# One mixer's scan pipelined by direction, with weight rounding on GpSimd and its remainder on VectorE

## The reference

```python
def step(s, inp):                       # one chunk of one head, one direction
    qc, kc, vc, gc = inp                # gc = log_sigmoid(z) / 16
    b = jnp.cumsum(gc, axis=2)
    b_last = b[:, :, -1:, :]
    q_dec = qc * jnp.exp(b)
    scores = jnp.where(mask, q_dec @ (kc * jnp.exp(-b)).T, 0.0)
    o = scores @ vc + q_dec @ s
    s_new = jnp.exp(b_last).T * s + (kc * jnp.exp(b_last - b)).T @ vc
    return s_new, o
```

```python
g = (gates.reshape(B, T, 4, HEADS) + b_gate).transpose(2, 0, 3, 1)
# log_i = g[0], g[2];  log_f = log_sigmoid(g[1]), log_sigmoid(g[3])
```

## Time and profile before

| | |
|---|---|
| median of 3 runs (lowest, highest) | 3000.23 us (2997.96, 3006.75) |
| the profiled execution | 3005.11 us, span 3003.2 us, mean granted TensorE clock 0.951 |
| TensorE busy | 2759.6 us, 92% of the span |
| VectorE, ScalarE, GpSimd busy | 1296.2, 986.0, 1001.6 us |
| first GLA projections start, scan of GLA head 0 starts | about 1603 us, about 1660 us |
| TensorE takes up the second half's scan | 2068.5 us |
| branch products begin | about 2350 us |

### The profile page before, as it was taken

How to read it: one execution, slowest core, us unless ns; L and a number is a source line. 1 busy time by engine, 2 the same in 40 slices (tenths; PEclk the granted TensorE clock), 3 DMA queues, 4 the chain that set the end, 5 groups by cost and what they waited for, 6 DMA issues and landing times.

```text
span 3003.2 us, 35461 instructions
## 1 busy us (share of the span) xinstructions
PE 2759.6 (92%) x13958; PEld 2141.7 (71%) x13958; DVE 1296.2 (43%) x1755; ACT 986.0 (33%) x1652; POOL 1001.6 (33%) x683
## 2 busy tenths in 40 slices
PE   7988999999999799999998888596998999899997
PEld 6866658887797574888876666465876565688886
DVE  2758445443354863544333344526333212333322
ACT  5468422222344872222223344322222100222221
POOL 5565403436545660134562322411220223200000
PEclk9999999999999999999998999797998999899998
DMA  5230024554422002355452111011111331233322
GB/s 127 91 65 1 19 70 119 148 134 133 140 75 84 18 1 59 104 137 139 133 145 66 43 29 42 28 29 28 43 43 42 80 88 57 65 104 95 88 87 67
DMA packets 386053, 230.39 MB, mean 77 GB/s; under 512 B 9340, under 2 KB 382204, under 8 KB 385888
## 3 DMA queue, kind: packets, MB, share of 16 engines
q1 hardware_dynamic: 383408, 224.09, 27.1%
q0 software_dynamic: 1952, 1.94, 0.8%
q10 hardware_dynamic: 528, 2.10, 0.2%
HBM read 226.01 MB, written 2.10 MB: 76 GB/s over the span
## 4 chain that ended last, share of the span: by engine, by line
PE 73%; DVE 9%; ACT 8%; DMA 6%; issue 2%; POOL 0%; SPq 0%; DVEq 0%; ACTq 0%; POOLq 0%
PE ps L815 63%; PE scores L815 7%; DMA raws<-in_w_down 5%; PE ps L957 1%; ACT wH L1770 1%; DVE R L2058 1%; DVE R L2316 1%; ACT R L1895 0%; DVE spare L2068 0%; ACT U L1609 0%; DMA ring<-in_w_in 0%; DVE R L2314 0%; DVE QK_parts L2048 0%; ACT spare L1632 0%; DVE R L2356 0%
## 5 line engine op out<-in xcount | busy, mean ns | idle before, releaser
L815 PE MATMUL ps<-xH,wH 128*128 128x512 f32 x1000 | 396.9, 397 | 8.3 <-DVE xL L2227 8.3
L815 PE MATMUL ps<-xL,wH 128*128 128x512 f32 x1000 | 391.3, 391 | 0.0
L815 PE MATMUL ps<-xH,wL 128*128 128x512 f32 x1000 | 390.9, 391 | 0.0
L1770 ACT ACTIVATE wH<-raws 128x2048 fp32r<-128x2048 f32 (+1 forms) x114 | 192.9, 1692 | 503.8 <-PE ps L815 307.3
L2253 DVE TENSOR_TENSOR wL<-raws,wH 128x2048 fp32r<-128x2048 f32 (+1 forms) x113 | 233.7, 2068 | 286.4 <-ACT wH L1770 286.3
L815 PE MATMUL ps<-ring_parts,U_parts 128*128 128x256 f32 (+1 forms) x1936 | 311.7, 290 | 12.8 <-DVE ring_parts L2110 6.2
L716 POOL TENSOR_TENSOR spare<-spare,cvec 128x1024 f32<-128x1024 f32 x64 | 124.5, 1946 | 563.6 <-DMA spare<-in_w_ada 563.6
L815 PE MATMUL ps<-R 128*64 128x128 f32 (+6 forms) x1768 | 276.6, 344 | 29.3 <-DVE R L2334 4.6
L815 PEld LDWEIGHTS ps<-ring_parts,U_parts 128*128 128x128 f32 x1936 | 277.7, 197 | 25.9 <-issue 22.6
L815 PEld LDWEIGHTS ps<-R 128*64 128x64 f32 (+2 forms) x1768 | 171.3, 166 | 131.1 <-issue 77.0
L768 POOL CAST ring_parts<-ring 128x2048 fp32r<-128x2048 f32 x28 | 54.6, 1951 | 547.5 <-DMA ring<-in_w_in 540.5
(11 more groups left out here) (408 smaller groups left out, 4697.5 us busy)
## 6 DMA issues: line engine op xcount, KB each, us to landing
raws<-in_w_gate_up SPq DMA_DIRECT2D x88, 512.0 KB, 5.5
ring<-in_w_in SPq DMA_DIRECT2D x34, 1024.0 KB, 5.9
spare<-in_w_ada SPq DMA_DIRECT2D x64, 512.0 KB, 4.1
raws<-in_w_down SPq DMA_DIRECT2D x32, 704.0 KB, 6.1
raws<-in_w_ffn_in SPq DMA_DIRECT2D x44, 512.0 KB, 5.1
ring<-in_w_in SPq DMA_DIRECT2D x22, 512.0 KB, 6.0
raws<-in_w_ffn_out SPq DMA_DIRECT2D x16, 704.0 KB, 4.5
ring<-in_w_o SPq DMA_DIRECT2D x6, 896.0 KB, 5.4
```

Of the source, the lines that this page charges most:

```text
L815: return nc.tensor.matmul(o, a, b, start=first, stop=last)
L1770: ap.do(f(wH[:, g % 2, 0:n], raws[:, g % 2, 0:n], ACT.Copy), wh_ready)
```

## The change

It has two parts.

**The decays of a direction are made during the scan of the one before.** `decays` is cut into `decay_sums` and `decayed`, `decay_exponents` into `decay_logs` and `decay_exponents`. In direction 0 of head h the decay inputs of (h, 1) go to TensorE behind the key transposes, and in direction 1 those of (h+1, 0). `q`, `k`, `v` 0 to 2 of the next head now lie in direction 0, and `v` 3 to 5 and both `gate` in direction 1, ahead of the outputs. `head_outputs` of head h-1 moves into direction 0 of head h, behind its second decay input; that of head 3 behind `q`, `k`, `k` of head 4. The decays of (0, 0) are made inside head 0's `v` projections. The minimum and the subtraction become one instruction.

**The gate rows of the second half** are biased, and their logarithms taken, on 16 x 768 before they are picked apart, inside direction 1 of head 3; the picked rows are then only copied.

**GpSimd only rounds (`round_piece`), and VectorE subtracts (`second_low`)** for pieces 1 to 23, at places written into VectorE's order; piece 0, the two small pieces and the branch and output pieces stay with GpSimd whole. GpSimd reorders five tiles and VectorE three.

The core of the diff; left out are names of semaphores and the places of scratch rows:

```diff
+            def round_piece(j):
+                i = PLACE[j]
...
+                pg.do(nc.gpsimd.tensor_copy(high, raw_), second_high)
...
             def gla_scan(h, d, nxt):
                 _, _, v_, _ = head(h)
+                last_head = h == NH2 - 1
...
                 key_transposes(kd[:, d, :])
                 transposed = ab.n
-                run(nxt("v", (2, 5)[d]))
+                if d == 0:
+                    decay_inputs(h, 1)
+                    if h > 0:
+                        head_outputs()
+                    run(nxt("v", 0) if last_head else nxt("q"))
+                    beside_states = nxt("v", 1) if last_head else nxt("k", 1)
+                elif last_head:
+                    pe.wait_ge(gates_split, 1)
+                    parts_job(ab, lambda b: b[0:16, 0:256], small(GATES_AT, 16), XcP)
+                    parts_job(ab, lambda b: b[0:16, :], small(GATES_AT, 16), XP)
+                    beside_states = nxt("gate", 0)
+                else:
+                    decay_inputs(h + 1, 0)
+                    run(nxt("v", 3))
+                    beside_states = chain(nxt("v", 4), nxt("v", 5))
                 pe.wait_ge(a_free, transposed)
...
+                if d == 0 and last_head:
+                    pp.more(u_permuted, 2)
+                    for m in range(2, 6):
+                        run(nxt("v", m))
+                elif d == 0:
+                    run(nxt("k", 0))
+                    for m in range(3):
+                        run(nxt("v", m))
+                elif last_head:
+                    run(nxt("gate", 1))
+                    pe.wait_ge(gates_logged, 1)
...
+                else:
+                    run(nxt("gate", 0))
+                    run(nxt("gate", 1))
...
             for h in range(NH2):
                 n_ = h + 1
...
+                if h > 0:
+                    head_norm(gla_squares)
+                keys_by_token(kdt)
+                decay_logs(h, 1)
                 if n_ < NH2:
...
+                    evacuate(n_, ("q", 0), ("k", 1), ("k", 0))
+                    decay_exponents(h, 1)
+                    evacuate(n_, ("v", 0), ("v", 1), ("v", 2))
...
+                if n_ < NH2:
+                    decay_logs(n_, 0)
+                    evacuate(n_, ("v", 3), ("v", 4), ("v", 5))
+                    decay_exponents(n_, 0)
+                    evacuate(n_, ("gate", 0), ("gate", 1))
...
+            def second_low(name, h):
+                j = SECOND.index((name, h))
+                raw_, high, low = place_parts(PLACE[j])
+                dve.wait_ge(second_high, j)
+                vp.do(v.tensor_tensor(low, raw_, high.bitcast(F32), ALU.subtract), piece_split)
...
+            second_low("v", 0)
+            decay_sums(0, 0)
+            decayed(0, 0)
+            second_low("gate", 0)
+            second_low("qk", 1)
             for h in range(NH2):
-                decays(h, 0)
+                vp.more(dec_ready)
+                masked(0)
+                if h > 0:
+                    head_outputs(h - 1, 3, Y)
+                second_low("v", h + 1)
                 if h == NH2 - 1:
...
                     for k in range(POOL_TILES, KT):
                         permute(vp, v, k, og_row)
                     vp.also(u_permuted)
...
+                states(gla_order(0), ST, DV, lambda c: dec[:, 0, c:c + 1])
+                decay_sums(h, 1)
+                decayed(h, 1)
+                if h == NH2 - 1:
+                    second_low("gate", NH2)
+                gla_outputs(0)
+                vp.more(dec_ready)
+                masked(1)
+                states(gla_order(1), ST, DV, lambda c: dec[:, 1, c:c + 1])
+                if h + 1 < NH2:
+                    second_low("gate", h + 1)
+                    decay_sums(h + 1, 0)
+                    decayed(h + 1, 0)
+                    if h + 2 < NH2:
+                        second_low("qk", h + 2)
+                else:
...
+                    second_low("qk", NH2)
+                gla_outputs(1)
+                vp.also(og_ready)
...
             rows(0)
+            head_outputs(NH2 - 1, 3, Y)
+            second_low("qk", NH2 + 1)
...
             rows(1)
+            second_low("v", NH2 + 1)
...
+                if d == 1 and h + 1 < NH2:
+                    second_low("gate", NH2 + h + 1)
...
                 if h + 1 < NH2:
+                    if h > 0:
+                        second_low("v", NH2 + h + 1)
                     convolve(h + 1)
                 for d in range(2):
                     mlstm_outputs(h, d)
+                vp.also(og_ready)
                 head_outputs(h, 4, YM)
+                if h + 2 < NH2:
+                    second_low("qk", NH2 + h + 2)
```

More of the change, by code:

```diff
@@ L779, in _ @@
             split_small(lr_in, LR_AT, 2 * RANK, lr_split)
[L780 to L784, removed]
+            def round_piece(j):
+                i = PLACE[j]
+                landed[i] += 16 * len(second_dmas(j))
+                pool.wait_ge(piece_in[i], landed[i])
+                raw_, high, _ = place_parts(i)
+                pg.do(nc.gpsimd.tensor_copy(high, raw_), second_high)
+            for j in range(1, SECOND.index(("gate", NH2))):
+                round_piece(j)
+                if j == 3:
+                    split_small(gates_in, GATES_AT, 16, gates_split)
             pool.wait_ge(head_in, NH2)
@@ L788, in _ @@
             pg.also(u_permuted)
-            for j in range(SECOND.index(("gate", NH2)), len(SECOND)):
+            for j in range(SECOND.index(("gate", NH2)), N_PROJ):
+                round_piece(j)
+            for j in range(N_PROJ, len(SECOND)):
                 split_piece(j)
@@ L1906, in _ @@
                 if n_ < NH2:
-                    evacuate(n_, ("k", 1))
-                evacuate(n_, ("v", 0), ("v", 1))
-                keys_by_token(kdt)
-                evacuate(n_, ("v", 2), ("v", 3), ("v", 4))
-                keys_by_token(kdt)
-                evacuate(n_, ("v", 5), ("gate", 0))
-                head_norm(gla_squares)
-                evacuate(n_, ("gate", 1))
-            act.wait_ge(y_ready, NH2)
-            bank = ab.take(act)
-            copy_out(G16[:, 0:256], bank[0:16, 0:256], a_free)
@@ L1920, in _ @@
-            bank = ab.take(act)
-            copy_out(G16[:, 256:768], bank[0:16, :], a_free)
-            evacuate(NH2, ("q", 0))
+                    evacuate(n_, ("q", 0), ("k", 1), ("k", 0))
+                    decay_exponents(h, 1)
+                    evacuate(n_, ("v", 0), ("v", 1), ("v", 2))
+                else:
+                    evacuate(n_, ("v", 0), ("v", 1))
+                    decay_exponents(h, 1)
+                    evacuate(n_, *[("v", m) for m in range(2, 6)])
+                keys_by_token(kdt)
@@ new lines, in _ @@
+                if n_ < NH2:
[3 more added lines that the diff above has]
+                    evacuate(n_, ("gate", 0), ("gate", 1))
+            for a, n in ((0, 256), (256, 512)):
+                bank = ab.take(act)
+                ap.do(f(G16[:, a:a + n], bank[0:16, 0:n], ACT.Identity, bias=bgate[:, 0:1]), a_free)
+            ap.do(f(LF16, G16, ACT.Abs))
+            ap.do(f(LF16, LF16, ACT.Exp, scale=-1.0))
@@ L1923, in _ @@
+            ap.do(f(LF16, LF16, ACT.Ln, bias=ones[0:16, 0:1]), gr_ln)
+            evacuate(NH2, ("gate", 0))
+            evacuate(NH2, ("gate", 1))
             for g in range(4):
@@ L1953, in _ @@
                 if h > 0:
-                    beside(("q", 0), ("k", 0), ("k", 1))
+                    beside(("q", 0))
+                    beside(("k", 0), ("k", 1))
                 beside(("v", 0))
```

113 lines of the change are left out of this document (47 added, 66 removed).

## The result

| | median (lowest, highest) | runs |
|---|---|---|
| before | 2999.1 us (2993.36, 3006.75) | 4 |
| after | 2962.44 us (2958.03, 2965.5) | 4 |

The ratio of after to before is 0.9875, with a 95% interval of 0.9849 to 0.9901: 36.7 us faster by the medians, 30 to 45 by the interval. Some 5 of the 47.0 lie where nothing was changed: the mixers begin 2.7 us earlier in the trace of after (1572.3 for 1575.0), and what follows the second half's scan is 2.0 us shorter.

What follows compares the result with a forecast made beforehand. TensorE, busy 92% of the span, was held by 86 us of waits between 1590 and 2070 us. Removing 82, adding 44 and regaining 12 by clock gives 50 us: 2955 from the profiled execution, 2950 against the median, range 2920 to 2984.

Steps and rivals of the forecast that it cites:

- The forecast case: Whole kernel: the named waits go and the listed smaller ones come, giving 2935 to 2972 us; chance 0.62.
- signs of being wrong: VectorE waiting for rounded pieces with states or outputs behind, clock staying at 0.92, or second half losing over 7 us.
- Waits removed: TensorE's waits: `q` 26.6 us, head 3's tiles 29.9, gate rows 22.2, and 3.3 of the opening's 7.4; together 82.0.
- Waits added before the gate rows: Opening 5 us, `v` of head 1 1.3, `head_outputs` 8, `gate`'s low part 2, head 3 11, gate rows 9.6.
- the tiles: Head 3, before the states: VectorE's three tiles take 11 us, so TensorE waits 6.3 us.
- The clock's 12 us: Heads 0 to 3 and behind the gate rows: work at 1.2 GHz speeds up, at most 14.5 us, taken as 12.
- The second half's 7 us: Second half: `q` twice waits for a low part behind `head_outputs`, 3.5 us each, 7 added.
- A: Added small waits are covered; only `head_outputs` (8) and the second half's `q` (7) remain: 81 us gained, 2920; chance 0.13.
- Rival B: VectorE and GpSimd hold each other up: 23 low parts each 1.9 us late, 44 lost, 2994; half, 2972; chance 0.14.
- C: Late loads stop the scan through VectorE's order: 2.2 us per piece uses up the gain, 4 gives 3042; chance 0.06.
- D: Decays still end last because VectorE reaches them only after the states: 3000 us; chance 0.05.
- The subtraction over 768 columns: On VectorE: 0.96 us everywhere in the profile after, where before it took 3.79 beside GpSimd's subtraction.

Runs made afterwards that it cites:

- e5: The changed kernel with only the second half's low part of `qk` moved ahead of `head_outputs`: 2945.73 us, ratio to before 0.9814.
- e9: e2 with only the second half's low part of `qk` moved ahead of `head_outputs`: 2981.45 us, ratio to before 0.9921.
- e1: The changed kernel, but GpSimd rounds and subtracts every piece and VectorE makes no low part: 2969.41 us, ratio to before 0.99.
- e2: The kernel before, old scan order, but GpSimd only rounds pieces 1 to 23 and VectorE subtracts: 2991.12 us, ratio to before 0.9965.
- e8: The changed kernel plus e5's edit, head 0's `v` 0 to 2 emptied before the first decay's exponents, and all eight tiles on GpSimd: 2939.94 us.
- e7: The changed kernel with ScalarE copying the transposed keys before the head norm in heads 1 to 3: 2973.11 us, ratio to before 0.9899.

## Why the prediction was right, and where its sum was off

**Range and sign.** 2950 was forecast, 2920 to 2984; it is 2962.4. The forecast case (2935 to 2972) holds: the waits it named went, and new ones came where it put them. But 37 to 41 us came of 50, and the sum came near by two errors that cancelled, which is luck. Two of its own signs of being wrong are there: the second half lost more than 7 us, and VectorE did wait for rounded pieces with states behind it, though that cost TensorE only 0.4.

**Waits removed.** 82.0 forecast. The `q`, tile and gate row waits are gone as listed, and the opening's 7.4 became 4.4: 3.0 against the 3.3 taken.

**Waits added before the gate rows**, forecast and measured: opening 5 and 5.6; `v` of head 1 1.3 and 0.4; `head_outputs` 3.5 and 2.7 each, and 1.4 once at L1341; `gate`'s low part 0.7 and 0.7 each; head 3's low part 4.7 and 4.3; the tiles 6.3 and 3.3; the gate rows 4.2 and 5.4, measured 4.4 and 4.8. With the 2.5 taken off as in the forecast, the sum is 31.9 for 36.9. The tiles are the largest difference: VectorE's three took 9.2 us (1896.55 to 1905.78), not 11. The forecast read the four of before as 5 us for the first and 2 to 5 for the others; its second took 6.3 (1930.35 to 1936.67), beside a GpSimd subtraction that the change takes away. The wait for the second input was put at L1299's successor and is in fact for the bank that ScalarE empties behind `head_norm`, the place the forecast gave as the further cause.

**The clock's 12 us failed.** The step was "half of the work that ran at 1.2 GHz", 2.5 us in each of three heads, 4 in head 3 and 3 at the gate rows. What ran low before was read rightly: TensorE was busy at 1.2 GHz for 5.2, 3.9 and 6.6 us in heads 0 to 2 and 8.9 in head 3. The forecast took it that with the waits gone none of it would remain. In heads 0 to 2 it fell to 0, 3.4 and 3.4, which gives 4.4 us back and not 7.5. In head 3 it rose to 18.2 at a clock of 0.87, which takes 4.6. Why, with shorter waits, is open. Over the whole stretch it is 44.3 us before and 43.8 after, so the clock gave nothing back. The rise of the mean clock is time that TensorE no longer spent waiting. The same work took 3 us more besides (busy time less half of its low part is 366.5 and 369.8), for which no run gives the reason.

What filled the place of the 12 is idle time: 55.1 us less, where 82 less 37 is 45. 5 of the difference are the new waits that came out smaller, and 4 are small waits for the states' banks, 7.6 us in twelve pieces before and 3.3 in six after, that the forecast did not count; 1 is left over. The forecast had 57 for this stage and A gives 52.1: 15 too much for busy time and 10 too little for idle time.

**The second half's 7 us was the other mis-sized term.** Its waits are right, 3.6 twice against 3.5. In the profiled pair the stage lost 9.9, 7.5 of it idle and 2.4 busy. By the means over all kernels it is 16, and by the runs of e5 and e9 13 to 18: the waits cost about their own length again through the clock. The forecast said that new waits "take a little" and netted that over the whole kernel; it belonged here, at full size.

**The rest is which execution was profiled.** 50 forecast, 47.0 in the profiled pair, 36.7 and 40.5 in medians. The stages give 52.1 less 9.9, so 42.2, and 4.7 of the 47.0 lie outside them, where the code is the same. The forecast took 4.9 us off for the level of the profiled before, but its terms came from that one trace.

**The rivals.** A: the small waits are there, so no. Rival B: VectorE and GpSimd do hold each other up, but the low parts pay next to nothing for it (the slowest took 2.57 us):

```profile
L2347 DVE TENSOR_TENSOR ring_parts<-ring,ring_parts 128x2048 fp32r<-128x2048 f32 x23 | 53.1, 2308 | 30.8 <-POOL ring_parts L785 29.3
```

23 of them at 2308 ns are 53.1 us, as forecast, and they waited 29.3 us in all for a rounding, in five places (16.68, 6.88, 1.86, 1.99 and 1.89). C: behind the 16.68, ahead of head 0's scan, TensorE lost nothing; behind the 6.88, in head 0's states, it lost 0.4, the `v` of head 1 above. Behind the other three I find no wait of TensorE. No load stopped the scan. D: no; e9 and e5 put the order at 32 to 36 us, and none of TensorE's waits in after is for a decay. The subtraction over 768 columns, forecast at 0.96 everywhere, was 2.07 once of eight, in the opening.

**The rule on the ports.** The earlier trace rows and the rows of e1 and of head 3 show each engine held by the other. The Trainium skill ("SBUF — State Buffer", Who interferes with whom) lists `tensor_scalar` and `copy` among the instructions that can take the shared pair, and says that the order of issue decides who is blocked. The traces agree. VectorE's four `tensor_scalar` took 3.67 us for 1.52, and its `copy` 4.76 for 0.59 in e1, where GpSimd's subtraction had begun 0.23 us before it. In head 3 of after the low part began first, at 1893.95, and GpSimd's copy behind it, at 1894.44, took 3.00 for 1.06.

## What to carry to other kernels

Ask of each small wait you add in what kind of stage it lies: in the opening, taking away 5.6 us of wait shortened the stage by 6.0, and in the second half's scan of small products 7.2 us of waits cost about twice their length. A mean clock that rises when waits go does not say that work became faster: compare the busy time first. Judge a change of two parts by stages as well as by the total, since e1 and e2 each hid 13 to 22 us under an opposite sign, and compare a stage with a second kernel that has the same code in it before you call a few us an effect. When work is moved from one engine to another, put it ahead of the chain that TensorE waits for only where the chain has slack: the same move won 13 to 18 us in one half and nothing in the other.

## What was not expected of the hardware

Waits of 3.6 us, two in a stage of 290 us, went with a lower granted clock over the stage: 0.83 to 0.86 with them and 0.86 to 0.89 without, and 16 us. A trace shows the stage moving between the two levels, 1.2 and 2.4 GHz, while TensorE is never idle; this is one stretch of 10 us of after:

```profile
2190.00:2200.00 10.00, 10.00 (x46) 9.20 (x46) 2.08 (x3) 3.28 (x5) 0.06 (x1) 0.55 0.00 0
```

and this one of e5:

```profile
2170.00:2180.00 10.00, 10.00 (x63) 8.05 (x61) 6.77 (x12) 1.58 (x3) 2.25 (x1) 1.00 0.38 107
```

They are not the same stretch of the program, and why the clock falls while TensorE is busy is open: no run varied that alone. What is shown is that the clock fell at both waits in all six traces that have them, and the association over thirteen traces, with e5 and e9 as the two pairs in which only the place of one low part differs. Kernels with the same code in this stage still differ by 7 us (273.1 in e5, 280.2 in e8) and by 9 (290.1 in after, 299.2 in e7), so a difference of a few us in it says nothing.
